# A hybrid decoder step: the sample-state products spread over four column groups of TensorE, and the norms' row scale applied when a tile leaves PSUM

## What is computed

```python
h = rmsnorm(x, g)                    # x * rsqrt(mean(x*x) + eps) * g
mix = even_mixer(h, ...)             # layer 0: 4 mLSTM heads and 16 SSD heads from ONE projection h @ w_in
x = x + mix
x = x + conv_ffn(rmsnorm(x, g2), ...)
mix = odd_mixer(rmsnorm(x, g3), ...) # layer 1: 8 retention heads with rotary q and k
...                                  # residual, norm, conv_ffn again, final rmsnorm

def conv_ffn(h, buf, w_up, conv_w, conv_b, w_down):
    u = h @ w_up                                     # 1024 -> 2 * 2816
    u, buf_new = causal_dwconv(u, buf, conv_w, conv_b)   # width 3, per channel
    gate, val = jnp.split(u, 2, axis=-1)
    return (jax.nn.silu(gate) * val) @ w_down, buf_new

num = einsum(s, v) + einsum('blhd,bhdv->blhv', q, C) * w_prev   # a head: C is the sample's own state
o   = einsum(s, v) + einsum('blhd,bhdv->blhv', q, S) * cross    # retention, the same shape of work
```

## Time and profile before

| | us |
|---|---|
| Median of 3 runs | 1119.96 |
| Lowest and highest run | 1118.69 and 1123.05 |
| Span of the profiled execution | 1115.8 |
| PE busy in it | 1098.7 |
| DVE busy | 736.3 |
| ACT busy | 525.0 |
| POOL busy | 299.2 |

### The profile page before, as it was taken

One profiled execution on the slowest core, in us unless ns is written; L12 is line 12 of the kernel. 1 busy time (PEld: TensorE's weight loads), 2 busy tenths in 40 slices (PEclk: granted clock), 3 DMA queues, 4 the chain that ended last, 5 costly groups with the idle time before them and its releaser, 6 DMA issues.

```text
span 1115.8 us, 19349 instructions
## 1 busy us (share of the span) xinstructions
PE 1098.7 (98%) x7385; PEld 1004.4 (90%) x7385; DVE 736.3 (66%) x1287; ACT 525.0 (47%) x1051; POOL 299.2 (27%) x473
## 2 busy tenths in 40 slices
PE   8999999999999999999999999999999999999997
PEld 7999996675579999999999999996669999999997
DVE  5465497755365699998447855435665399999542
ACT  6456655333144555555335333545443465555432
POOL 2000154324011055544002530003542035545100
PEclk9999998966699999999999999999999999999999
DMA  8635345430335355455553744445654435445541
GB/s 297 238 114 189 121 155 168 169 104 19 104 125 177 99 182 170 156 170 174 182 169 115 264 163 149 160 161 166 214 186 159 154 126 176 155 169 170 185 152 43
DMA packets 64685, 177.19 MB, mean 159 GB/s; under 512 B 5889, under 2 KB 24065, under 8 KB 64593
## 3 DMA queue, kind: packets, MB, share of 16 engines
q1 hardware_dynamic: 64160, 174.11, 47.0%
q0 software_dynamic: 432, 1.85, 0.4%
HBM read 154.88 MB, written 21.05 MB: 158 GB/s over the span
## 4 chain that ended last, share of the span: by engine, by line
PE 94%; DVE 3%; ACT 1%; DMA 1%; issue 1%; SPq 0%; DVEq 0%; ACTq 0%
PE gemm L655 24%; PE gemm L657 23%; PE gemm L656 23%; PE mix L783 4%; PE mix L750 2%; PE gemm L679 2%; PE mix L895 1%; PE mix L719 1%; PE mix L729 1%; PE gemm L736 1%; PE gemm L794 1%; PE gemm L685 1%; PE mix L751 1%; DMA vec<-vecs 1%; PE mix L749 1%
## 5 line engine op out<-in xcount | busy, mean ns | idle before, releaser
L1332 DVE TENSOR_TENSOR wl<-raw,wh 128x1024 fp32r<-128x1024 f32 x257 | 315.1, 1228 | 218.2 <-ACT wh L982 206.4
L655 PE MATMUL gemm<-hH,wh 128*128 128x288 f32 x1512 | 451.0, 298 | 0.8 <-DVE wl L1332 0.8
L656 PE MATMUL gemm<-hL,wh 128*128 128x288 f32 x1512 | 446.7, 295 | 0.0
L657 PE MATMUL gemm<-hH,wl 128*128 128x288 f32 x1512 | 445.2, 294 | 0.0
L982 ACT ACTIVATE wh<-raw 128x1024 fp32r<-128x1024 f32 x257 | 271.0, 1057 | 154.8 <-PE gemm L657 148.2
L655 PEld LDWEIGHTS gemm<-hH,wh 128*128 128x128 f32 x1512 | 284.0, 188 | 2.0 <-issue 1.2
L657 PEld LDWEIGHTS gemm<-hH,wl 128*128 128x128 f32 x1512 | 285.3, 189 | 0.0
L656 PEld LDWEIGHTS gemm<-hL,wh 128*128 128x128 f32 x1512 | 284.6, 188 | 0.1
L1477 DVE SCALAR_TENSOR_TENSOR cy<-pad,vec,cy 128x304 f32<-128x304 f32 (+1 forms) x212 | 132.6, 625 | 7.5
L657 PE MATMUL gemm<-HH,wl 128*128 128x288 f32 x352 | 104.4, 296 | 0.0
L655 PE MATMUL gemm<-HH,wh 128*128 128x288 f32 x352 | 104.0, 296 | 0.0
(11 more groups left out here) (323 smaller groups left out, 1483.7 us busy)
## 6 DMA issues: line engine op xcount, KB each, us to landing
raw<-wts SPq DMA_DIRECT2D x257, 512.0 KB, 3.3
st<-r_in SPq DMA_DIRECT2D x9, 512.0 KB, 5.8
r_out<-st SPq DMA_DIRECT2D x9, 512.0 KB, 4.0
st<-c_in SPq DMA_DIRECT2D x8, 514.0 KB, 5.6
c_out<-st SPq DMA_DIRECT2D x8, 514.0 KB, 3.9
sts<-h_in SPq DMA_DIRECT2D x12, 256.0 KB, 3.5
h_out<-sts SPq DMA_DIRECT2D x12, 256.0 KB, 2.6
st3r<-r_in SPq DMA_DIRECT2D x4, 512.0 KB, 5.8
```

What stands on the lines that cost most here:

```text
L655: mm(out, h, xh, start=(k == 0), stop=False)
L656: mm(out, h, xl, start=False, stop=False)
L657: last = mm(out, lo, xh, start=False, stop=(k == K - 1))
L1332: do(tt(wl[:, c % RING, :], raw[:, c % RING, :], wh[:, c % RING, :].bitcast(F32), ALU.subtract), lo_ready)
```

## The change

The edit has two parts.

**Sample-state products in four column groups.** The eight products of `oi` (and of `si`) no longer all add into partitions 0 to 31. Sample b goes to the 32 partitions of group b % 4, so that two products are added in each group. ACT scales all 128 partitions into `num`, and a new fp32 matmul with a constant 128 x 32 matrix `fold` adds the four groups up, into the same bank as `os`. `oi` moves to the front of the head's work. For the SSD part the folding matmul is a job of its own, `sf`.

**The norms' row scale at the evictions.** The projections now run on x times gain, without rstd; hH comes from ACT directly from x (a copy with a scale), hL from DVE in one operation. Both are made as each output tile is added to x. The squares are added up by POOL, PE does one matmul with ones in place of eight, after the first two tiles, and the 18 matmuls without use are gone. Every tile is then multiplied by rstd as it leaves PSUM, which DVE does for all kinds; ACT's Sigmoid and Silu follow in place. In exchange the first tap of the convolutions moves from DVE to ACT, and the product of gate and value from DVE to POOL. The start of the program loads the gains before the constants and runs 8 such idle matmuls in place of 4 and 9.

The core of the diff:

```diff
 # jobs of a head, and the products
+            job(f"{kind}oi{h}", "act")
             job(f"{kind}o0{h}", "act")
...
-            job(f"{kind}oi{h}", "act")
...
-                    last = mm(out[0:NS, 0:w], qTm[:, hg % 2, b, :], state(n)[:, b % 4, 0:w],
-                              start=(b == 0), stop=(b == NB - 1))
+                    last = mm(out[QUAD[b % 4], 0:w], qTm[:, hg % 2, b, :], state(n)[:, b % 4, 0:w],
+                              start=(b < 4), stop=(b >= 4))
...
-                mm(out[0:NS, 0:w], s[0:NS, TP + P:BLK], va(2)[0:NS], start=True, stop=True).then_inc(mix_done, 1)
+                mm(out[0:NS, 0:w], s[0:NS, TP + P:BLK], va(2)[0:NS], start=True, stop=False)
+                wait_empty(pe, f"{kind}oi{h}")
+                mm(out[0:NS, 0:w], fold, num[:, hg % 2, 2, 0:w], start=False, stop=True).then_inc(mix_done, 1)
...
 # PE: norm and the first tiles
             def norm(n):
                 out = free_bank(f"norm{n}")[:, 0:T]
-                for i in range(KD):
-                    pe.wait_ge(sq_ready, KD * n + i + 1)
-                    last = mm(out, ones, hF[:, i, :], start=(i == 0), stop=(i == KD - 1))
-                last.then_inc(mix_done, 1)
+                pe.wait_ge(ssq_ready, n + 1)
+                mm(out, ones, hF[:, 0, :], start=True, stop=True).then_inc(mix_done, 1)
...
             def ffn(l):
-                norm(2 * l + 1)
-                t0 = START[f"up{l}"]
-                first_tiles(t0, 2 * l + 1)
+                n, t0 = 2 * l + 1, START[f"up{l}"]
+                tiles([t0, t0 + 1], operand_of(n), (xlo_ready, KD * n))
+                norm(n)
...
 # ACT: squares and high parts with each output tile, first taps
+            def high_and_square(n, i):
+                if n < 4:
+                    s.do(act(H[n][0][:, i, :], xT[:, i, :], ACT.Copy, scale=v(f"norm{n}", i)), xhi_ready)
+                s.do(act(hF[:, i, :], xT[:, i, :], ACT.Square), sq_ready)
...
+            def first_tap(n, t, x, width, tap, bias):
+                wait_tile_empty(eng, t)
+                eng.wait_ge(fill_done, n + 1)
+                s.do(act(cy[:, n % 4, 0:width], x[:, 0:width], ACT.Identity, scale=tap, bias=bias), tap_done)
...
                             split(last_chunk(t0 + i) + 3)
-                            wait_tile(eng, t0 + i)
                             n = XB + 2 * KF * l + i
-                            ...
-                            s.do(act(p[:, W2:W2 + TP], b[:, 0:TP], ACT.Copy))
-                            s.do(act(padded(p, W2)[:, :, W2:], smp(b), ACT.Copy), gemm_act)
+                            if x and j >= 2:
+                                eng.wait_ge(hid_ready, KF * l + j - 1)
+                            first_tap(n, t0 + i, pad[:, n % 4, 1:], 304, v("fcw", (2 * KF * l + i) * 3),
+                                      v("fcb", 2 * KF * l + i))
                     if 1 <= j <= KF:
                         silu(j - 1)
                     if j >= 2:
                         high(j - 2)
...
 # DVE: low parts, evictions, the FFN
+            def low(n, i):
+                eng.wait_ge(xhi_ready, KD * n + i + 1)
+                hi, lo = H[n]
+                do(stt(out=lo[:, i, :], in0=xT[:, i, :], scalar=v(f"norm{n}", i), in1=hi[:, i, :].bitcast(F32),
+                       op0=ALU.mult, op1=ALU.subtract), xlo_ready)
...
+            def scaled_rows(t, n, x, w):
+                wait_tile(eng, t)
+                if n >= 4:
+                    eng.wait_ge(tail_done, n - 3)
+                b = bank[t % 4]
+                do(tt(x[:, w:w + TP], b[:, 0:TP], rstd[:, 0:TP], ALU.mult))
+                do(tt(padded(x, w)[:, :, w:], smp(b), smp(rstd), ALU.mult), gemm_dve)
...
             def ffn(l):
...
+                for i in range(2 * KF + 1):
+                    if i < 2 * KF:
+                        split(last_chunk(t0 + i) + 3)
+                    if i == 0:
+                        eng.wait_ge(rstd_ready, 2 * l + 2)
+                        eng.wait_ge(zeroed, 4 + 2 * l)
+                    else:
+                        m = i - 1
+                        convolve(n0 + m, pad[:, (n0 + m) % 4, 1:], 304, [v("fcw", (2 * KF * l + m) * 3 + d) for d in range(3)])
+                    if i < 2 * KF:
+                        scaled_rows(t0 + i, n0 + i, pad[:, (n0 + i) % 4, 1:], W2)
...
 # POOL
+            def sum_squares(n):
+                for i in range(1, KD):
+                    eng.wait_ge(sq_ready, KD * n + i + 1)
+                    if i > 1:
+                        settle()
+                    do(tt(hF[:, 0, :], hF[:, 0, :], hF[:, i, :], ALU.add), ssq_ready if i == KD - 1 else None)
```

More of the change, by code:

```diff
@@ L119, in parts @@
             t += 1
[L122 to L128, removed]
 JOBS = []
@@ L765, in middle @@
                 s = Sp[:, hg % 2, :]
+                out = free_bank(f"{kind}oi{h}")
+                pe.wait_ge(qm_ready, hg + 1)
+                for b in range(NB):
+                    n = 2 * hg + b // 4
+                    pe.wait_ge(st_in[n % SLOTS], 16 * (n // SLOTS + 1))
+                    last = mm(out[QUAD[b % 4], 0:w], qTm[:, hg % 2, b, :], state(n)[:, b % 4, 0:w],
+                              start=(b < 4), stop=(b >= 4))
+                last.then_inc(mix_done, 1)
                 wait_empty(pe, f"{kind}sc{h}")
@@ L839, in _ @@
             pe.wait_ge(blank, 1)
-            for _ in range(4):
+            for _ in range(WARM):
                 mm(bank[0][:, 0:T], rstd[:, 0:P], rstd[:], start=True, stop=True)
-            pe.wait_ge(const_in, 16)
-            norm(0)
-            first_tiles(T0, 0)
+            tiles([T0, T0 + 1], operand_of(0), (xlo_ready, 0))
             for t in range(T0 + 2, START["even_out"]):
@@ L854, in _ @@
                     row_max(2)
-                tiles([t], normed)
+                tiles([t], operand_of(0))
+                if t == T0 + 2:
+                    pe.wait_ge(const_in, 16)
+                    norm(0)
                 if 9 <= t <= 16:
@@ L894, in si, with sf @@
                     pe.wait_ge(sts_in[n % SSLOTS], 16 * (n // SSLOTS + 1))
-                    last = mm(out[0:NS, :], cm[:, g, b, :], sts[n % SSLOTS], start=(b == 0), stop=(b == NB - 1))
+                    last = mm(out[QUAD[b % 4], :], cm[:, g, b, :], sts[n % SSLOTS], start=(b < 4), stop=(b >= 4))
                 last.then_inc(mix_done, 1)
+            def sf(g):
+                out = free_bank(f"sf{g}")
+                pe.wait_ge(si_ready, g + 1)
+                mm(out[0:NS, :], fold, itmp[:, :], start=True, stop=True).then_inc(mix_done, 1)
             def sp_(g):
@@ L1146, in ffn @@
                         high(j - 2)
-                for i in range(KD):
-                    split(last_chunk(START[f"down{l}"] + i) + 3)
+                out_tiles(f"down{l}", 2 * l + 2)
             def gate_exponentials():
@@ L1723, in _ @@
             back("r", CH - 1)
-            out_tiles("odd_out", 2)
+            out_tiles("odd_out", 3)
             ffn(1)
-            norm(4)
+            eng.wait_ge(rstd_ready, 5)
+            for i in range(KD):
+                do(stt(out=hF[:, i, :], in0=xT[:, i, :], scalar=v("norm4", i), in1=rstd[:],
+                       op0=ALU.mult, op1=ALU.mult), y_ready)
         @block.gpsimd
```

341 lines of the change are left out of this document (165 added, 176 removed).

## The result

| | before | after |
|---|---|---|
| Median, us | 1121.51 (4 runs) | 1273.59 (4 runs) |
| Span of the profiled execution, us | 1115.8 | 1272.1 |
| PE, DVE, ACT, POOL busy, us | 1098.7, 736.3, 525.0, 299.2 | 1107.0, 735.2, 532.3, 337.5 |
| Mean granted clock of PE | 0.966 | 0.919 |

The changed kernel takes 1.134 times as long, with a 95% interval of 1.129 to 1.139. The forecast was +110 us; the span grew by 156. The direction and the mechanism were right, the size was not: 1273.6 lies above the stated range of 1195 to 1265.

A forecast was written before the change was run, and what follows sets the result against it. The prediction took PE as the bound, with DVE close behind. Its terms, 0 + 27 - 1 - 4.5 + 52.5 - 5.9 - 9 + 52.5 - 1.3, made +110.3; with 1115.8 and 4.2 that gave 1230 us, range 1195 to 1265.

The forecast's parts named there:

- the ring in the up tiles: Up tiles: DVE eviction, ACT tap, wh, wl, two taps wait in a circle, 4.18 or 4.86 us; +52.5 us per FFN.
- What bounds the kernel: Whole kernel: PE, busy 98% of 1115.8 us, is the bound; DVE is close behind in the up tiles.
- the hold of DVE by POOL in a rival: Up tiles: no circle of waits, but POOL's added product holds DVE; 1090 to 1104 us, chance 0.04.
- The ends of the up stage: Each FFN: first eviction at X + 8.0, X being the last output tile's end; last eviction to first down tile 5.3 us.
- The allowance of 2 us for the clock: Each FFN: 2 us added for matmuls at 1.2 GHz and one late chunk.
- The even projection: Even projection: +27 us, of it +21.1 from xbc tiles waiting in a circle of 5.2 us a tile.
- the ring of "3.1 us, just under a tile's 3.2": og and z tiles: eviction, Silu in place, wh, wl take 3.1 us; ACT's work there starts the xbc tiles 2.4 late.
- Norms: Norm before the odd projection -5.9 us, last norm -1.3 us, start of the program 0.
- Sample-state products: Heads and SSD part: 16 records in 2.0 us instead of 3.58; retention heads -9, SSD -4.5, mLSTM heads -1 us.
- The rival with four groups fully side by side: Sample-state products: full overlap, gaining 2.2 us a head and 5.1 each SSD; 14 us less, 1216 us, chance 0.16.
- The clock falls in the ring: Up and xbc tiles: PE works only 3.2 of 4.5 us, so its granted clock falls; 1263 us, chance 0.07.
- The ring does not bind: Tiles' serial part stays under 3.2 us, so the gains stand alone: 33.5 us less, 1086 us, chance 0.05.

The follow-up runs named there:

- a term doubled: The changed kernel with ACT doing each first tap of the up tiles twice: 1330.0 us.
- the column groups alone: The kernel before with only the sample-state products in four column groups and their folds, norms and evictions as before: 1105.8 us, ratio 0.986.
- the pair order: The kernel before with only the four column groups, a head's products issued in sample order 0, 4, 1, 5, 2, 6, 3, 7: 1103.6 us.
- all rings opened: The changed kernel with ACT's wh conversion moved ahead of its wait for DVE in up, og, z, xbc, rg and 16-block output tiles: 1086.7 us.
- the norm part alone: The changed kernel without its column-group part, products in one group at their old place: 1290.5 us, ratio 1.150.
- the ring open: The changed kernel with ACT converting chunk i+4 before the first tap of tile i, in both FFNs' up tiles: 1120.4 us.

## Why the prediction was right in kind and short in size

What failed is the size of the sum, above all the length of the ring in the up tiles. The prediction had 193.0 us for the 43 distances of an FFN and its range allowed them to be 0.1 us longer each; they were 0.36 longer each, 208.4.

- **What bounds the kernel.** Right. PE was the bound before, and the count of work per engine was no guide: DVE's busy time fell a little (736.3 to 735.2), where the forecast had counted 0.4 us less a pair in the up tiles.
- **The ring in the up tiles.** Right, and shown from three sides: opened, it gives back 153 us; a term doubled, every distance grows by that term; without the tap on ACT it isn't there. Its length was mis-sized in two terms. The tap until ACT's next operation took 0.54 to 0.55 us (470.40 to 470.95), not 0.34: I had priced it by a Silu of the same size, and this operation takes scale and bias from a column each. Other rows point the same way: a plain ACT copy of 288 columns (HH) takes 0.43, one with a scale from a column (hH) 0.54. That is 0.20 a tile, 9 us an FFN. And POOL's new product pushes POOL's HL into the wl, which takes 1.49 to the next start in place of 1.16, 0.33 a pair, 7 us an FFN. Together 16, against the 15.4 us by which the 43 distances (208.4) exceeded my 193.0. I had used the hold of DVE by POOL in a rival and left it out of my own sum.
- **The ends of the up stage.** The first eviction came at X + 6.8 (forecast 8.0). From the last eviction to the first down tile it was 9.65 us, where I had 5.3. Two things were missing. POOL's last product and HL stood behind POOL's other work, so PE finished that tile 7.4 us after the last eviction (at 632.9). Then the addition waited 2.2 us more, since three conversions stand ahead of it in DVE's program:

```profile
631.74 3.50 DVE L1303 TENSOR_TENSOR wl<-raw,wh 128x1024 fp32r<-128x1024 f32 x3 [3.50 <-ACT wh L963]
635.15 0.45 DVE L1319 TENSOR_TENSOR xT<-gemm,xT 128x288 f32<-128x288 f32 x1
```

  The same stretch was 8.7 us before (520.31 to 529.04), but there it was PE's own work: the 66 matmuls of the tile began at 520.11 and the last one ended at 529.00. PE goes on with the next tile while the addition waits, so part of these 2.2 us comes back in the down tiles (60.42 us in place of 61.08). The allowance of 2 us for the clock went into this: 15.4 - 1.2 + 4.3 - 2 = 16.5 for each FFN, the 16.4 measured.
- **The even projection.** The xbc ring was right (5.37 us a tile against 5.2; the tap again). The stretch ahead of it was not: 12.2 us late, forecast 4.8. With the rings of og and z opened, that stretch came back by 9.7. I read it so: the ring of "3.1 us, just under a tile's 3.2" had no slack left for the table changes, the gate exponentials and the weights that ACT does in the same place. Which of these took how much wasn't tested, and the clock of the next point has a part in it.
- **A clock term that no part of the sum had.** At the small products of the gate columns the granted clock fell to half in some executions. Busy times by stretch (PE, PEld, DVE, ACT, POOL; then clock, DMA), first before, then the column groups alone:

```profile
120.00:125.00 5.00, 5.00 (x35) 4.56 (x35) 1.23 (x1) 3.90 (x8) 0.00 (x0) 1.00 0.01 3
```

```profile
120.00:125.00 5.00, 5.00 (x19) 3.77 (x18) 0.85 (x1) 3.51 (x8) 0.00 (x0) 0.50 0.00 0
```

  There the twelve xbc tiles began 4.7 us later (139.23 against 134.50). With the pair order, which has the same work at this place, the same window shows 1.00 and the tiles began at 133.62, so it needn't be a cost of the column groups. All the traces with the norm part have it: in the changed kernel the clock was 0.50 from 125 to 130, after PE had been busy for only 3.31 of the 5 us before. With all rings opened it is there too (0.50 from 120 to 125), and the xbc tiles still began 2.9 us later than before. The four executions of the column groups alone fall into two pairs, 1108.4 and 1109.3 us with a mean clock of 0.949, 1102.8 and 1103.2 with 0.955. The clock is part of why the spans of like kernels differ (1106.7 and 1096.9) by more than their medians (1105.8 and 1103.6).
- **Norms.** The odd projection and its heads together gained 17.9, 5.9 + 9 forecast. With the column groups alone they gained 13.3, which leaves 4.6 for the norm; with the norm part alone they gained 5.3. The last norm gained 0.8 (1.3).
- **Sample-state products.** The gain per head was under-priced: 3.58 - 1.07 - 0.45 = 2.1 us, and the period of a head fell from 10.2 to some 8.2. The rival with four groups fully side by side was right on this point. Over eight heads 13.3 came of 16.8; in some, PE now waits up to 0.7 us for the load of a state. In the SSD part and the mLSTM heads together the gain was 0.5 with the column groups alone and 1.1 in the changed kernel (1.4 to 2.6 in the runs that open or alter its rings, 4.4 with the pair order), and not 5.5. From 175 to 325 us the granted clock is low in all of them, but lower with the change: its mean is 0.76 before, 0.69 with the column groups alone and 0.72 with the pair order. In the changed kernel two of the four mLSTM heads' products ran at half speed (1.94 us), and the wait for the second head's state, which the forecast named, took 6. How the missing 5 us divide between clock and wait wasn't settled. That the part as a whole was forecast at 14.5 us (9 + 4.5 + 1) and gave 14.5 alone is luck: one miss covered the other.
- **The output tiles.** Forecast at nothing. They have a ring of their own (addition, ACT's high part and square, wh, wl): 3.54 us a tile in the even and odd output against 3.17 by PE. It cost 1.1 us each; opening it gave that back.
- **The rivals.** "The clock falls in the ring" was partly there: 0.93 and 0.96 in the two up stages (450 to 520 and 1010 to 1090 us), 1.00 before. It is a result of the gaps: with the ring open it is 1.00. "The ring does not bind", 1086, is what the kernel does once its order is changed, 1086.7. The order in ACT's program decided, but that the two numbers meet is partly luck: that trace gained 17.9 us in the odd projection and its heads, and up to the first even addition it was 4.1 us slower than before, where the count had a gain. The chances didn't quite add up either: the two rivals that end faster than before have 0.05 + 0.04, where the summary gives 0.07.

## What to carry to other kernels

When work moves between two engines that already pass something back and forth, write down the circle: which operation waits for which, and what stands ahead of it in each program. Its length from start to start, not the engines' busy time, is the new pace, and here moving one conversion ahead of one wait turned +13% into no change, and the same in the other stages made it -3%. Price each term by a row with the same operands, follow the end of a stage through each engine's program, and count contention on the path once it is known to exist.

## What the runs showed of the hardware that was not expected

- Products in four column groups of TensorE ran side by side almost fully, 16 records in 1.07 us at full clock against 3.58 to 3.65 in one group and 1.92 in two, and their order in the program made no difference (1.07 and 1.09). The Trainium skill (TensorE: Matmul & The Clock Gate, Part 3) gives 2.38 times for three column tiles; here four gave 3.3 to 3.4.
- An Identity on ACT with scale and bias from columns took 0.64 us for 304 columns, 0.54 to the next start; a Silu without them 0.44 and 0.35. The function differs too, and no run separates the two.
- DVE and POOL held each other in both directions: a POOL copy of 16 columns took 1.20 us beside a wl (it ended at 474.32, the wl at 474.26) and 0.21 beside an eviction, and three DVE taps took 2.67 in place of 1.55.
